# A two-block network on one core: input loads in another order, MLP squares inside the last quarter, stores in pieces, tiles moved to 64-word places, context additions on GpSimd

## What is computed

```python
def rmsnorm(x, g):
    return x * lax.rsqrt(jnp.mean(x * x, axis=-1, keepdims=True) + RMS_EPS) * g

# first block, layer l
h = rmsnorm(x, norm_mix_pre[l]);  ... h @ w_in[l] ...
mem_n = rmsnorm(mem, norm_memkv[l])
x = x + rmsnorm(memory_cross_attention(h, mem_n, ...), norm_mem_post[l])

# second block, layer l (last: l == 1)
x = x + g1_x * rms_norm(m_x, norm_g[l, 1])
f_x = squared_relu_mlp(modulate(rms_norm(x, norm_g[l, 2]), sh2_x, sc2_x), w_mlp_in[l], w_mlp_out[l])
x = x + g2_x * rms_norm(f_x, norm_g[l, 3])
if not last:
    ctx = ctx + g1_c * rms_norm(m_c, norm_g[l, 1])
    f_c = squared_relu_mlp(...)
    ctx = ctx + g2_c * rms_norm(f_c, norm_g[l, 3])
```

## Time and profile before

| | |
|---|---|
| median of 3 runs | 3855.02 us (3854.51 to 3859.83) |
| the profiled execution, its own time | 3854.92 us |
| its span in the profile | 3853.1 us |
| mean granted TensorE clock | 0.985 |
| PE / PEld / DVE / ACT / POOL busy | 95% / 77% / 52% / 39% / 6% |
| chain that ended last, by engine | PE 82%, DVE 7%, ACT 6% |

### The profile page before, as it was taken

The page is one execution under the profiler, slowest core; times in us unless marked ns, Lnnn a source line. Parts: engine busy times, 40 slices in busy tenths (PEclk is TensorE's granted clock), DMA queues, the critical chain, the costliest instruction groups (busy, mean ns, idle before and its releaser), DMA issues.

```text
span 3853.1 us, 52811 instructions
## 1 busy us (share of the span) xinstructions
PE 3642.8 (95%) x19430; PEld 2974.7 (77%) x19430; DVE 2007.3 (52%) x3383; ACT 1508.5 (39%) x2303; POOL 241.6 (6%) x384
## 2 busy tenths in 40 slices
PE   7999989999999998899999888899999898889997
PEld 5788877887787887688778776788888787668885
DVE  4634466777763445677773565433233344644443
ACT  4344354332324535533244366422122335742322
POOL 0000000001000000000000151000000002610000
PEclk9999999999999999999999999999999999999999
DMA  3222222446322223144541101111111121212222
GB/s 124 98 72 88 96 85 82 146 140 199 114 98 77 83 99 104 55 142 147 192 133 61 44 12 31 44 60 60 66 61 65 38 71 49 30 44 92 93 93 71
DMA packets 112574, 333.14 MB, mean 86 GB/s; under 512 B 32680, under 2 KB 33576, under 8 KB 111784
## 3 DMA queue, kind: packets, MB, share of 16 engines
q1 hardware_dynamic: 73472, 264.18, 20.5%
q0 software_dynamic: 14400, 52.44, 4.2%
q10 hardware_dynamic: 24552, 14.51, 1.7%
HBM read 328.99 MB, written 6.00 MB: 87 GB/s over the span
## 4 chain that ended last, share of the span: by engine, by line
PE 82%; DVE 7%; ACT 6%; issue 2%; DVEq 1%; POOL 0%; ACTq 0%; POOLq 0%; DMA 0%; SPq 0%
PE PS L595 14%; PE PS L597 13%; PE PS L596 13%; PE PS L970 11%; PE PS L969 10%; PE PS L972 10%; PE PS L670 2%; PE PS L1097 1%; PE PS L756 1%; ACT PB L1653 1%; ACT FULL_P L1653 1%; ACT L1351 1%; PE PS L768 1%; DVE Y L2345 1%; DVE WL L1887 1%
## 5 line engine op out<-in xcount | busy, mean ns | idle before, releaser
L1887 DVE TENSOR_TENSOR WL<-RAW,WH 128x1024 fp32r<-128x1024 f32 x494 | 604.5, 1224 | 572.1 <-ACT WH L1315 565.5
L1315 ACT ACTIVATE WH<-RAW 128x1024 fp32r<-128x1024 f32 x494 | 521.4, 1056 | 658.2 <-PE PS L972 369.2
L595 PE MATMUL PS<-HHI,WH 128*128 128x512 f32 x1632 | 645.8, 396 | 25.2 <-DVE HLO L1924 17.5
L597 PE MATMUL PS<-HHI,WL 128*128 128x512 f32 x1632 | 641.9, 393 | 0.0
L596 PE MATMUL PS<-HLO,WH 128*128 128x512 f32 x1632 | 641.0, 393 | 0.0
L969 PE MATMUL PS<-H2HI,WH 128*128 128x512 f32 (+1 forms) x1336 | 471.2, 353 | 0.0
L970 PE MATMUL PS<-H2LO,WH 128*128 128x512 f32 (+1 forms) x1336 | 450.4, 355 | 0.0
L595 PEld LDWEIGHTS PS<-HHI,WH 128*128 128x128 f32 x1632 | 307.0, 188 | 109.9 <-issue 23.4
L972 PE MATMUL PS<-H2HI,WL 128*128 128x512 f32 (+1 forms) x1336 | 387.8, 350 | 0.0
L596 PEld LDWEIGHTS PS<-HLO,WH 128*128 128x128 f32 x1632 | 307.4, 188 | 66.1 <-issue 0.5
L597 PEld LDWEIGHTS PS<-HHI,WL 128*128 128x128 f32 x1632 | 307.3, 188 | 64.6
(11 more groups left out here) (350 smaller groups left out, 5769.0 us busy)
## 6 DMA issues: line engine op xcount, KB each, us to landing
RAW<-in_stream SPq DMA_DIRECT2D x494, 512.0 KB, 3.3
MODW<-in_modw POOLq DMA_DIRECT2D x96, 512.0 KB, 3.6
bias_rows<-in_rpb ACTq DMA_DIRECT2D x8, 476.2 KB, 6.6
MEM<-in_mem ACTq DMA_DIRECT2D x3, 1024.0 KB, 4.7
X<-in_x SPq DMA_DIRECT2D x1, 2048.0 KB, 9.1
CROW<-in_crow POOLq DMA_DIRECT2D x4, 512.0 KB, 4.6
out<-X SPq DMA_DIRECT2D x1, 2048.0 KB, 7.1
BIAS<-bias_rows ACTq DMA_DIRECT2D x8, 224.0 KB, 4.8
```

The lines of the kernel that those rows point to most:

```text
L595: nc.tensor.matmul(out, WH[:, slot, b * P:(b + 1) * P], hi, start=start, stop=False)
L597: return nc.tensor.matmul(out, WL[:, slot, b * P:(b + 1) * P], hi, start=False, stop=stop)
L1315: A(WH[:, d, :], RAW[:, s, :], ACT.Copy).then_inc(high_split, 1)
L1887: TT(WL[:, d, :], RAW[:, s, :], WH[:, d, :].bitcast(F32), ALU.subtract).then_inc(split_ready, 1)
```

## The change

- **Start.** `X` comes in four DMAs with a semaphore each (`x_part`), in front of `PAR`; `MEM` is SP's last load of the start instead of ACT's first. ACT preloads the table for Ln and squares `X` as the pieces land. The squares of `MEM` go to a tile of their own (`MEM_SQ`) after the first norm's `norm_high`; PE adds them after the first `chunk_pair` (`memory_sums`), and ACT takes the root straight into `MR` (`memory_root`) just ahead of the two `Sin`.
- **MLP end.** The fourth quarter is taken out of the loop on ACT and DVE. ACT squares each block of `Y2` when DVE has added its last part, DVE adds the squares into `ACC`, and PE runs `statistics` in the place of `sum_squares`.
- **Stores.** `out` is written in five pieces, each after its own blocks.
- **Places.** `at2` is rounded up to a multiple of 64 words from `Z` in front of `H2LO`.
- **Residual.** DVE scales the context's part first and `x`'s second, and adds `x` alone. GpSimd adds the context (`context_added`), one block at a time behind `ctx_go`; ACT's squares wait for `ctx_ready` as well.

```diff
@@ places
+        MEM_SQ = place("MEM_SQ", [P, KB, TC], at=ZB + KB * T)
...
+        at2[0] = Z + -(-(at2[0] - Z) // 64) * 64
         H2LO = place2("H2LO", [P, KB, TA], F32R)
@@ sync
-            sp.dma_start(X[:], x).then_inc(x_in, 16)
-            sp.dma_start(PAR[:], params1).then_inc(x_in, 16)
+            for j in range(4):
+                sp.dma_start(X[:, 2 * j:2 * j + 2, :], x[:, 2 * j:2 * j + 2, :]).then_inc(x_part[j], 16)
+            sp.dma_start(PAR[:], params1).then_inc(par_in, 16)
...
+            sp.dma_start(MEM[:], mem).then_inc(mem_in, 16)
...
-            sp.wait_ge(x_ready, DEPTH * 3 * KB + DEPTH * 2 * KB)
-            sp.dma_start(out.rearrange("(k p) t -> p k t", p=P), X[:]).then_inc(stored, 16)
-            sp.wait_ge(stored, 16)
+            result = out.rearrange("(k p) t -> p k t", p=P)
+            pieces = ((0, 2), (2, 4), (4, 6), (6, 7), (7, 8))
+            for k0, k1 in pieces:
+                sp.wait_ge(x_ready, DEPTH * 3 * KB + DEPTH * 2 * KB - KB + k1)
+                sp.dma_start(result[:, k0:k1, :], X[:, k0:k1, :]).then_inc(stored, 16)
+            sp.wait_ge(stored, 16 * len(pieces))
@@ gpsimd
+            def context_added(residuals):
+
+                for k in range(KB):
+                    pool.wait_ge(ctx_go, residuals * KB + k + 1)
+                    nc.gpsimd.tensor_tensor(CTX[:, k, :], CTX[:, k, :], Y2[:, k, T:TA], ALU.add).then_inc(ctx_ready, 1)
+                pool.drain()
+
+            context_added(0)
             zero_outputs(0)
+            context_added(1)
@@ tensor
-            pe.wait_ge(x_in, 16 * 4)
-            sum_squares(TC, 0)
+            def memory_sums():
+
+                for k in range(KB):
+                    m.add("sq")
+                    pe.wait_ge(sq_ready, m.at("sq"))
+                    nc.tensor.matmul(FLAT[:, 6 * T:6 * T + TC], ONES[:], MEM_SQ[:, k, :], start=k == 0, stop=k == KB - 1).then_inc(sq_summed, 1)
+
+            pe.wait_ge(ones_in, 32)
             sum_squares(T, 0)
...
                 chunk_pair(HHI, HLO)
+                if l == 0:
+                    memory_sums()
...
-                sum_squares(TA if full else T)
+                statistics(TA if full else T)
@@ scalar
+            act.preload_act_table(ACT.Ln)
+            act.wait_ge(ones_in, 32)
             squares_summed(of_x0, T)
             for _ in range(SPLIT_AHEAD):
                 split_high()
-            act.wait_ge(mr_ready, 1)
             root(T, summed=True)
...
                 norm_high()
+                if l == 0:
+                    memory_squares()
                 for c in range(2):
                     take(U[:, c, :].unsqueeze(1))
                 if l == 0:
-
+                    memory_root()
                     act.wait_ge(ang_ready, 1)
...
+                hidden_high()
+                for k in range(KB):
+                    p = unit_wait()
+                    split_high()
+                    m.add(f"use{p}")
+                    dst = square_slot(k)
+                    act.wait_ge(taken[p], m.at(f"use{p}", 1))
+                    A(dst[:, 0:n2], Y2[:, k, 0:n2], ACT.Square, scale=D ** -0.5).then_inc(y_squared, 1)
+                m.add("sqt", KB - 1)
                 act.preload_act_table(ACT.Ln)
-                squares_summed(of_y3, n2)
-                root(n2, summed=True)
+                root(n2)
@@ vector
-                        for v, c in spans(full):
-                            STT(Y2[:, b, c], Y2[:, b, c], MOD[:, l * MODS + part * KB + b, v:v + 1], RS[:, c], ALU.mult, ALU.mult)
+                        for v, c in reversed(spans(full)):
+                            last = STT(Y2[:, b, c], Y2[:, b, c], MOD[:, l * MODS + part * KB + b, v:v + 1], RS[:, c], ALU.mult, ALU.mult)
+                            if v:
+                                last.then_inc(ctx_go, 1)
                     dve.drain()
                     for b in (k, k + 1):
-                        for v, c in spans(full):
-                            last = TT(xpart(v)[:, b, :], xpart(v)[:, b, :], Y2[:, b, c], ALU.add)
-                        last.then_inc(x_ready, 1)
+                        TT(X[:, b, :], X[:, b, :], Y2[:, b, 0:T], ALU.add).then_inc(x_ready, 1)
...
+                hidden_squared()
+                for k in range(KB):
+                    output_added(slice(k, k + 1), k % 2)
+                    if k < KB - 1:
+                        split_low()
+                    if k:
+                        add_squares(k - 1, n2, y_square_arrived)
+                add_squares(KB - 1, n2, y_square_arrived)
+                split_low()
```

More of the change, by code:

```diff
@@ L414, in build @@
         high_split, split_ready, units_done = sem("high_split"), sem("split_ready"), sem("units_done")
-        x_in = sem("x_in")
+        ones_in, par_in, x_part = sem("ones_in"), sem("par_in"), [sem(f"x_part{j}") for j in range(4)]
         taken = [sem("taken0"), sem("taken1")]
@@ L438, in build @@
         y_zero = sem("y_zero")
+        ctx_go, ctx_ready = sem("ctx_go"), sem("ctx_ready")
         probs_summed, probs_inverse = sem("probs_summed"), sem("probs_inverse")
@@ L1400, in attention, with memory_squares, memory_root @@
                     A(PTS[:, n % 2, 0:n_keys], FLAT[:, 4 * T:4 * T + n_keys], ACT.Copy).then_inc(pts_ready, 1)
-            act.dma_start(MEM[:], mem).then_inc(mem_in, 16)
-            act.wait_ge(x_in, 16 * 4)
-            act.wait_ge(mem_in, 16)
-            def of_mem(k, dst, n):
-                A(dst[:, 0:n], MEM[:, k, :], ACT.Square, scale=D ** -0.5).then_inc(sq_ready, 1)
-            squares_summed(of_mem, TC)
             def of_x0(k, dst, n):
+                if k % 2 == 0:
+                    act.wait_ge(x_part[k // 2], 16)
                 A(dst[:, 0:n], X[:, k, :], ACT.Square, scale=D ** -0.5).then_inc(sq_ready, 1)
-            root(TC, summed=True)
+            def memory_squares():
+                act.wait_ge(mem_in, 16)
+                for k in range(KB):
+                    A(MEM_SQ[:, k, :], MEM[:, k, :], ACT.Square, scale=D ** -0.5).then_inc(sq_ready, 1)
+                m.add("sum", KB)
+            def memory_root():
+                act.wait_ge(sq_summed, m.at("sum"))
+                inverse_root(MR[:], FLAT[:, 6 * T:6 * T + TC]).then_inc(mr_ready, 1)
+            act.preload_act_table(ACT.Ln)
+            act.wait_ge(ones_in, 32)
             squares_summed(of_x0, T)
@@ L1613, in spans, with squares_x @@
                 return ((0, slice(0, T)), (1, slice(T, TA)))[:2 if full else 1]
-            def squares_x(full, ctx_first):
+            def squares_x(full, ctx_first, residuals=0):
                 for k in range(KB):
@@ L1624, in squares_x @@
                     if full and not ctx_first:
+                        act.wait_ge(ctx_ready, (KB if residuals else 0) + k + 1)
                         A(dst[:, T:TA], CTX[:, k, :], ACT.Square, scale=D ** -0.5)
@@ L1841, in _, with hidden_high @@
                 norm_high2(l, 3, full)
-                with m.loop(act, QUARTERS, units=2 * KB, use0=KB, use1=KB, val=KB, w=2 * KB, **{name: 2 * KB // RAW_SLOTS for name in RAW_LAPS}):
+                def hidden_high():
                     with m.loop(act, KB // 4, units=4, use0=2, use1=2, val=4, **QUAD) as i:
@@ L1851, in _ @@
                             A(GHI[:, bass.ds(4 * i + c, 1), 0:n2], TMP[:, p:p + 1, 0:n2], ACT.Copy).then_inc(hi_ready, 1)
+                with m.loop(act, QUARTERS - 1, units=2 * KB, use0=KB, use1=KB, val=KB, w=2 * KB, **{name: 2 * KB // RAW_SLOTS for name in RAW_LAPS}):
+                    hidden_high()
                     with m.loop(act, KB // 4, units=4, **QUAD):
@@ L1983, in _ @@
             nc.vector.memset(DEN[:], 0.0).then_inc(taken[1], 1)
-            dve.wait_ge(x_in, 16 * 4)
+            dve.wait_ge(ones_in, 32)
+            dve.wait_ge(par_in, 16)
             m.add("sq", 2 * KB)
-            m.add("root")
-            dve.wait_ge(root_ready, m.at("root"))
-            nc.vector.tensor_copy(MR[:], RS[:, 0:TC]).then_inc(mr_ready, 1)
             for _ in range(SPLIT_AHEAD):
@@ L2535, in _, with hidden_squared @@
                 dve.wait_ge(y_zero, l + 1)
-                with m.loop(dve, QUARTERS, units=2 * KB, use0=KB, use1=KB, relu=KB, hi=KB, w=2 * KB, **{name: 2 * KB // RAW_SLOTS for name in RAW_LAPS}):
+                def hidden_squared():
                     with m.loop(dve, KB // 4, units=4, use0=2, use1=2, relu=4, hi=4, **QUAD) as i:
```

35 lines of the change are left out of this document (19 added, 16 removed).

## The result

The changed kernel takes 3810.6 us (median of 4 runs, 3807.56 to 3812.82) against 3855.11 before (3854.51 to 3859.83). The ratio is 0.9881, 95% interval 0.9864 to 0.9898. It is faster by 44.5 us.

The account below looks back on a forecast made before the run. PE's stream of weight products was taken as the bound. Start -11.7, MLP ends -17.4, stores -3.8, residuals +4.2 and places -7 sum to -35.7: 3855.0 - 35.7 = 3819.3 us, range 3802 to 3835.

Parts of the forecast that it names:

- Start: Start of the kernel: `X` loaded first, Ln table preloaded, `x`'s root 16.5 us earlier; net -11.7 us, bounds -8 and -13.
- What the `Sin` gave back: At the start: the memory's root in front of the two `Sin` makes the chain to PE's weights at 60.23 late by 4.8 us.
- MLP ends: Second block's two MLP ends, last stream product to Ln: 14.5 us becomes 4.8, 11.5 becomes 3.8; -9.7 and -7.7 us.
- Stores: Last store: `out` lands in 7.1 us, a last piece of 256 KB in 3.1; -3.8 us, bounds -3 and -4.5.
- Residuals: Two residuals with a context: GpSimd's additions and DVE take turns at SBUF; +4.2 us for both, ends -4.7 and +8.
- Places: Second block's stream matmuls: moving the tiles shortens each product; -7 us, taken between 0 and -18.
- The stretch at 233 ns on aligned tiles: First block's own MLP, 345 matmuls in 80 us; the prediction's reason to take a tile-move gain nearer to nothing.
- 1: Rival, residuals: GpSimd's additions hide after all; 3819.3 - 8.9 = 3810.4 us, chance 0.18.
- 2: Rival, residuals: DVE starves GpSimd, one addition a pair; +4 us a residual, +8, time 3823, chance 0.16.
- 3: Rival, second block's stream: the move of the tiles does nothing; 3826.3 us, chance 0.17.
- 4: Rival, second block's stream: the move of the tiles brings all it can, -18 at most; 3808 us, chance 0.09.
- 5: Rival, whole stream: pitch is a state of the program and the new one is slow everywhere; 3864 us, chance 0.03.

## Why the prediction was right, and where it was not

- **What bounds the kernel**: right. All that was won was won where PE had no stream work, or in the pitch of the stream.
- **Start**, forecast -11.7, measured -8.9. `x`'s root was forecast 16.5 us earlier and came 14.6 earlier. Two steps failed. The first piece of `X` landed later than the "3.3 us" of a weight unit (first square at 5.86, not 5.1: 0.8). And the squares to the root were taken to last as before: PE's sums of `x` took 9.1 us then, behind those of the memory, and take 10.2 now as PE's first work (1.1), since the first seven of the sixteen take about 0.85 us each and the rest 0.43 to 0.53 (rows below). What the `Sin` gave back was forecast as 4.8 and is 4.1. Missing altogether is the clock behind that wait, 1.6: a wait of PE was priced at its length only. The prediction's own range for that chain was mis-added: 4.2 plus the table load of 1.3 is 5.5, not 6.5.

  Stretches of the changed kernel at its first sums (columns as above, the first count is PE's):

```profile
7.00:10.00 3.00, 3.00 (x4) 1.06 (x4) 0.00 (x0) 0.64 (x2) 0.00 (x0) 1.00 1.03 405
...
14.00:17.00 3.00, 2.86 (x7) 0.78 (x6) 0.23 (x1) 2.58 (x4) 0.00 (x0) 1.00 0.95 334
```

  Four sums in 3 us, then seven. The profile's clock reads 1.00 in both, though the lengths are those of its two levels (1.2 and 2.4 GHz); the kernel with matmuls ahead of the sums, which takes the slow length away, is what shows that it is the clock.
- **MLP ends**, forecast -9.7 and -7.7, measured -9.6 and -7.7. Read from a stretch of the same kernel that already worked the other way.
- **Stores**, forecast -3.8, measured -5.0. The term was sized by a load of 256 KB into SBUF (3.1 us); a store of that size lands in 2.1. By its own rows the forecast would have been 7.1 - 3.1 = 4.0; it gives no reason for the 0.2 less.
- **Residuals**, forecast +4.2, measured +2.0. The mechanism, that the two engines take turns, was right, the size was not: each addition costs DVE 0.42 us, not 0.65, a figure that the prediction does not work out. It is close to the whole of the 0.73 us it gave the addition; DVE pays only for the part that is left when its next instruction starts, less 0.14 to 0.20. The length was mis-sized the other way, 1.17 instead of 0.73 from a line between two other shapes. Two slips stand in the sum as well: the 0.3 us at the end of ACT's squares should have been added and not taken off (measured +1.0 a residual: 0.7 in the four pairs and 0.3 behind them), and twice 2.2 is 4.4.
- **Places**, forecast -7, measured -13.5 (the kernel without the rounding). The step that failed is the discount "nearer to nothing because of that stretch". The stretch at 233 ns on aligned tiles was real, but another thing. Counted with the pitches by units, 2.1 ns on 3264 matmuls, 1.2 on 1536, 1.5 on 1152 and 5.4 on 768 give 14.6 us. The "about 234", "230" and "175" of the prediction are not the plain quotients of the earlier trace rows (232.6, 227.5 and 173.7), which count matmuls cut at the edges; the pitches by units bear them out.
- **The Trainium skill's form for the pitch** ("TensorE: Matmul & The Clock Gate", section "Back-to-back issue gap"), which would have made this term 0, does not hold here, neither in its value (216 against 228.9) nor in having no term for places. The page gives that form for an isolated matmul, and about 131 ns for 512 columns in a stream of weight loads and matmuls; the trace agrees with neither.
- **Sum**: 2.8 too much for the start, against 6.5, 2.2 and 1.2 too little for places, residuals and stores; 7.1 of the 8.7 us. The rest is less than the spread of the runs. That the start erred the other way than the other three is luck; with the start right the forecast would have been 11.5 us off.
- **Rivals**. 1 gave the right time for a wrong reason: its -4.7 us would have been a pair of blocks at 3.5, and it is 4.33. 2 is out, since GpSimd's additions start 0.57 us after DVE's first scaling and none takes more than 1.18 us. 3 is out by the kernel without the rounding. 4 named -18, and -13.5 is nearer to it than to the forecast. 5 is out as told, but a slow pitch that comes and goes does exist.
- **Signs**. Of those that the prediction named for being right, two did not come: `x`'s root before 19 us (DVE's copy behind it is at 20.27) and PE's load of 60.23 some 11 to 12 us earlier (it is 10.5). The others did, the longer DVE instructions by 0.37 and 0.46 instead of 0.6.

## What to carry to other kernels

Price a gap of the bottleneck twice: its length, and the clock that PE may lose in it. Try the places of a matmul stream's tiles: a shift of the moving tiles to multiples of 256 bytes from those of the first block cost 160 bytes a partition and was worth 0.35% here. Which distance matters is open, so in another kernel the fast place has to be found by trying. Moving element work from DVE to GpSimd beside DVE's own two-input instructions was no offload: compare what DVE saves (0.34 us) with what the other engine takes from it (0.42), which is less the less is left of the GpSimd instruction when DVE's next one starts. And a total that agrees with a forecast or a rival shows nothing about it until each term has been read in its own place.
